# A hybrid decoder block on one core: five runs of small products a period, new engine orders, and three sums by ones as pairs of f32r products

## What is computed

```python
h = layer_norm(concat([meta, x]), ln_in_g, ln_in_b)
p = h @ w_in[l]
ya = rwkv7_branch(...)     # time mixer, 32 heads of 64
yb = pool_branch(...)      # causal pooling, windows 2, 4, 8, 16
merged = gate[:, :, 0] * (ya @ w_branch_a[l]) + gate[:, :, 1] * (yb @ w_branch_b[l])
h = layer_norm(DN_ALPHA * h + merged @ w_out[l], ln1_g[l], ln1_b[l])
h = layer_norm(DN_ALPHA * h + peer_ffn(h, ...), ln2_g[l], ln2_b[l])
```

```python
kk = kk / jnp.maximum(jnp.linalg.norm(kk, axis=-1, keepdims=True), 1e-12)
yv = jnp.mean(jnp.square(y - ym), axis=-1, keepdims=True)
bonus = jnp.sum(r_h * k_h * r_k, axis=-1, keepdims=True) * v_h
```

## Time and profile before

| | |
|---|---|
| median of 3 runs | 2405.33 us (2404.95 to 2405.37) |
| the profiled execution, its span | 2404.5 us |
| TensorE busy over the span | 2157.6 us (90%) |
| VectorE busy over the span | 1529.0 us (64%) |
| ScalarE busy over the span | 684.3 us (28%) |
| GpSimd busy over the span | 659.7 us (27%) |
| first and last transpose of V_st (`t`, once a pair) | 89.8 and 615.4 us |
| first product of the merge | 681.3 us |
| granted TensorE clock over the span | 0.992 of full |

### The profile page before, as it was taken

One profiled execution on the slowest core, in us unless ns is written; L12 is line 12 of the kernel. 1 busy time (PEld: TensorE's weight loads), 2 busy tenths in 40 slices (PEclk: granted clock), 3 DMA queues, 4 the chain that ended last, 5 costly groups with the idle time before them and its releaser, 6 DMA issues.

```text
span 2404.5 us, 37848 instructions
## 1 busy us (share of the span) xinstructions
PE 2157.6 (90%) x15331; PEld 1510.5 (63%) x15331; DVE 1529.0 (64%) x2605; ACT 684.3 (28%) x1366; POOL 659.7 (27%) x539
## 2 busy tenths in 40 slices
PE   9999999999999999998999889978877787777776
PEld 8999999999899999987554444433332233222222
DVE  7778888888765455548876567667446444444445
ACT  6555555455344444432121111111011000000000
POOL 1000000000000000004554555555455445444442
PEclk9999999999999999999999999999999999999999
DMA  6533333333367666679999999999999999999997
GB/s 213 141 95 98 102 88 101 103 88 98 106 184 194 185 187 187 190 270 342 417 427 424 425 423 426 427 427 426 427 427 428 426 427 427 427 427 427 427 427 289
DMA packets 348320, 708.19 MB, mean 295 GB/s; under 512 B 13834, under 2 KB 272482, under 8 KB 281826
## 3 DMA queue, kind: packets, MB, share of 16 engines
q0 software_dynamic: 74176, 537.01, 53.1%
q1 hardware_dynamic: 273732, 168.55, 24.1%
q10 hardware_dynamic: 240, 0.22, 0.0%
HBM read 703.63 MB, written 2.10 MB: 294 GB/s over the span
## 4 chain that ended last, share of the span: by engine, by line
DMA 36%; PE 17%; issue 2%; DVE 2%; POOL 1%; DVEq 0%; ACT 0%; POOLq 0%; ACTq 0%
DMA query_w<-in_v_table,experts 17%; DMA rows<-in_v_table,experts 13%; PE bank L1980 7%; PE project L1980 4%; DMA rows<-in_u_table,experts 3%; DMA up_rows<-in_u_table,experts 3%; PE bank L247 2%; DMA down_row_more<-in_v_table,experts 2%; PE bank L1896 2%; PE project L247 1%; PE bank L1938 0%; PE bank L1944 0%; PE bank L1612 0%; PE bank L1923 0%; POOL rows L1851 0%
## 5 line engine op out<-in xcount | busy, mean ns | idle before, releaser
L2102 DVE CUSTOM_DVE_ANT_0 rows<-rows,h 128x2048 f32<-128x2048 f32 x170 | 388.7, 2292 | 329.7 <-DMA rows<-in_u_table,experts 329.5
L1851 POOL DMA_INDIRECT rows<-in_u_table,experts x170 | 182.9, 1076 | 1097.7 <-DVE experts L1449 1040.0
L232 DVE TENSOR_TENSOR w_half_rest<-w_half,w_half_high 128x1024 fp32r<-128x1024 f32 x224 | 271.4, 1219 | 160.5 <-ACT w_half_high L211 160.3
L247 PE MATMUL project<-hT_high,w_half_high 128*128 128x272 f32 (+1 forms) x1152 | 351.1, 305 | 0.4 <-PEq L254 0.3
L1980 PE MATMUL bank<-query_w,merged_spare 128*128 128x512 f32 x608 | 283.6, 602 | 60.7 <-DMA query_w<-in_v_table,experts 47.3
L1980 PE MATMUL bank<-rows,merged_spare 128*128 128x512 f32 x612 | 286.4, 605 | 57.2 <-DMA rows<-in_v_table,experts 43.8
L247 PE MATMUL project<-hT,w_half_high 128*128 128x272 f32 (+1 forms) x1152 | 329.2, 286 | 0.0
L247 PE MATMUL project<-hT_high,w_half_rest 128*128 128x272 f32 (+1 forms) x1152 | 328.7, 285 | 0.0
L2102 DVE CUSTOM_DVE_ANT_0 up_rows<-up_rows,h 128x2048 f32<-128x2048 f32 x86 | 197.0, 2292 | 168.7 <-DMA up_rows<-in_u_table,experts 168.7
L211 ACT CAST w_half_high<-w_half 128x1024 fp32r<-128x1024 f32 x224 | 234.9, 1051 | 204.3 <-PE merge_ps L247 120.6
L1980 PEld LDWEIGHTS bank<-rows,merged_spare 128*128 128x128 f32 x612 | 114.0, 192 | 223.2 <-issue 127.3
(11 more groups left out here) (435 smaller groups left out, 3760.3 us busy)
## 6 DMA issues: line engine op xcount, KB each, us to landing
w_half<-in_w_in SPq DMA_DIRECT2D x176, 512.0 KB, 4.1
w_half<-in_w_branch_a SPq DMA_DIRECT2D x32, 512.0 KB, 3.9
out_w<-in_w_out SPq DMA_DIRECT2D x16, 1024.0 KB, 5.6
w_half<-in_w_branch_b SPq DMA_DIRECT2D x16, 512.0 KB, 3.9
query_w<-in_w_q_peer SPq DMA_DIRECT2D x8, 1024.0 KB, 16.2
out_w<-in_w_q_peer SPq DMA_DIRECT2D x6, 1024.0 KB, 19.1
lora_weights<-in_w_in SPq DMA_DIRECT2D x4, 896.0 KB, 14.1
rows<-in_u_table,experts POOLq DMA_INDIRECT x170, 21.1
```

Source lines behind the costliest of these rows:

```text
L232: return eng.tensor_tensor(low.bitcast(F32R), x, high, ALU.subtract)
L247: mm = nc.tensor.matmul(out, a.bitcast(F32R), b.bitcast(F32R), start=start and n == 0, stop=stop and n == 2)
L1851: pool.indirect_dma_start(ur[n % RU], None, w["u_table"][0], bass.IndirectOffsetOnAxis(ap=k.idx[:, t, h, j:j + 1], axis=0)).then_inc(s_u[n ...
L2102: v.tensor_tensor_reduce(ur[n % RU], ur[n % RU], k.h[:, n // (HEADS * TOPK), :], 1.0, 0.0, ALU.mult, ALU.add, dots(n, n + 1)).then_inc(s_d ...
```

## The change

Three things are done together.

1. *The three sums by ones.* `head_sums` makes each as two f32r products of a 128x128 matrix of ones, one with the rounded high part and one with the rest. ScalarE writes the high part (a second square in `sq` and `yc`, a copy in the new `bk`), VectorE the rest (`kq`, `br`, `gq`), and TensorE waits for the rest (`ksplit`, `rksplit`, `ysplit`).
2. *New orders for three engines.* TensorE has five runs of small products a period where it had seven. `u` of chunk c, `T` and `s` now stand in one run; before, `u` closed a run and `s` opened the next. `gv` goes from the end of stage 3 to the next period, between `Z` and `lw`. `gr` is cut in two with `s` 4, `T` 5 and `t` between them. On VectorE `go` moves from ahead of `s` 0 to behind `T` 1; `e` 2 moves ahead of `s` 0, `e` 0 ahead of `s` 2.
3. *Work moved between engines.* Two affine steps go from VectorE to ScalarE (the second line of `lw`, the new `lt`), and the per-pair copies of the parameter vectors (`cv`, and the first line of `ge`) are gone: operations read `k.vec` itself.

The diff, cut to its core (of the orders one line each):

```diff
 PE_ORDER = (
-    ("t", 1, 2), ("rb", 0, 2), ("u", 0, 3), ("lw", 0, 1), ("f", 10, 0), ("s", 0, 3), ("Z", 1, 2), ("r", 1, 3), ("la", 0, 1),
+    ("t", 1, 2), ("u", 0, 3), ("Z", 1, 2), ("gv", 0, 4), ("lw", 0, 1), ("f", 10, 0),
...
 DVE_ORDER = (
+    ("go", 0, 4), ("split", 3, 0), ("la", 0, 1), ("s", 1, 3), ("r", 2, 3), ("T", 2, 2), ("gy", 0, 4), ("lk", 0, 1), ("kq", 0, 1), ("split", 4, 0), ("e", 0, 0),
...
+            def head_sums(out, high, rest):
+
+                nc.tensor.matmul(out, ones_high[:].bitcast(F32R), high.bitcast(F32R), start=True, stop=False)
+                return nc.tensor.matmul(out, ones_high[:].bitcast(F32R), rest.bitcast(F32R), start=False, stop=True)
...
             def nm(_, p, par):
                 wait(pe, q["sig"], p * 3 + 3)
-                wait(pe, q["ksq"], p + 1)
-                nc.tensor.matmul(low[:, 0:T], ones, sq[:, real], start=True, stop=True).then_inc(q["norm"], 1)
+                wait(pe, q["ones"], 1)
+                wait(pe, q["ksplit"], p + 1)
+                head_sums(low[:, 0:T], sq_high[:], sq_rest[:, real]).then_inc(q["norm"], 1)
...
-            def gr(_, p, par):
+                wait(pe, q["rksplit"], p + 1)
+                head_sums(low[:, 0:SEQ], rk_high[:], rk_rest[:, CH:TP]).then_inc(q["bonus"], 1)
+
+            def gr(i, p, par):
 
                 wait(pe, q["st"], p + 1)
-                wait(pe, q["kst"], p + 1)
-                wait(pe, q["Zst"], p * 5)
-                wait(pe, q["off"], p)
-                for n, lhs in ((0, bst), (2, kst)):
-                    for c in range(NCH):
-                        mm = by_head(inv[n][:, c * CH:(c + 1) * CH], lhs[:, c, :], ast[par][:, c, :])
-                    mm.then_inc(q["gram"], 1)
+                if i:
+                    wait(pe, q["kst"], p + 1)
+                    wait(pe, q["Zst"], p * 5)
+                else:
+                    wait(pe, q["off"], p)
+                for c in range(NCH):
+                    mm = by_head(inv[2 * i][:, c * CH:(c + 1) * CH], (bst, kst)[i][:, c, :], ast[par][:, c, :])
+                mm.then_inc(q["gram"], 1)
...
+                if c == 1:
                     wait(pe, q["vsqrt"], p)
...
             def gv(_, p, par):
-                wait(pe, q["sqr"], p + 1)
-                nc.tensor.matmul(var_ps, ones, ysq[:], start=True, stop=True).then_inc(q["var"], 1)
+                wait(pe, q["ysplit"], p + 1)
+                if p + 1 < PAIRS:
+                    wait(pe, q["Uc"], p * 5 + 6)
+                head_sums(var_ps, ysq_high[:], ysq_rest[:]).then_inc(q["var"], 1)
...
             def sq_(_, p, par):
                 wait(act, q["shifted"], p * 3 + 3)
                 wait(act, q["norm"], p)
-                nc.scalar.activation(sq[:, real], kx[par][:, real], ACT.Square, scale=cur[par][:, V_KK:V_KK + 1]).then_inc(q["ksq"], 1)
+                nc.scalar.activation(sq[:, real], kx[par][:, real], ACT.Square, scale=k.vec[:, V_KK, p:p + 1])
+                nc.scalar.activation(sq_high[:].bitcast(F32R), kx[par][:, real], ACT.Square, scale=k.vec[:, V_KK, p:p + 1]).then_inc(q["ksq"], 1)
+
+            def bk(_, p, par):
+                wait(act, q["bonus"], p)
+                wait(act, q["rk"], p + 1)
+                nc.scalar.copy(rk_high[:].bitcast(F32R), rk[:, CH:TP]).then_inc(q["rkr"], 1)
 
             def lw(_, p, par):
                 wait(act, q["csum"], p)
                 wait(act, q["lora_mm"], p * 3 + 1)
-                nc.scalar.activation(sg[:, real], low[:, 0:T], ACT.Tanh, scale=0.5, bias=cur[par][:, V_W0H:V_W0H + 1]).then_inc(q["sig"], 1)
+                nc.scalar.activation(sg[:, real], low[:, 0:T], ACT.Tanh, scale=0.5, bias=k.vec[:, V_W0H, p:p + 1]).then_inc(q["sig"], 1)
+                wait(act, q["sig"], p * 3 + 1)
+                nc.scalar.activation(sg[:, real], sg[:, real], ACT.Copy, scale=0.5, bias=0.5).then_inc(q["sg"], 1)
...
+            def lt(_, p, par):
+                wait(act, q["rk"], p)
+                wait(act, q["sig"], p * 3 + 2)
+                nc.scalar.activation(t1[:, real], am[:, real], ACT.Identity, scale=k.vec[:, V_KAH, p:p + 1],
+                                     bias=k.vec[:, V_KAC, p:p + 1]).then_inc(q["rate"], 1)
...
             def y(_, p, par):
                 wait(act, q["done"], p)
                 wait(act, q["Yo"], p * 4 + 4)
-                nc.scalar.activation(ysq[:], y_ps, ACT.Square).then_inc(q["sqr"], 1)
+                nc.scalar.activation(ysq[:], y_ps, ACT.Square)
+                nc.scalar.activation(ysq_high[:].bitcast(F32R), y_ps, ACT.Square).then_inc(q["sqr"], 1)
                 nc.scalar.copy(yc[:], y_ps).then_inc(q["Yc"], 1)
...
+            nc.scalar.copy(ones_high[:].bitcast(F32R), ones).then_inc(q["ones"], 1)
...
-            def cv(_, p, par):
-                d()
-                n.tensor_copy(cur[par][:], k.vec[:, :, p]).then_inc(q["rm"], 1)
+            def kq(_, p, par):
+                wait(dve, q["ksq"], p + 1)
+                rest_bits(n, sq_rest[:, real], sq[:, real], sq_high[:]).then_inc(q["ksplit"], 1)
+
+            def br(_, p, par):
+                wait(dve, q["rkr"], p + 1)
+                rest_bits(n, rk_rest[:, CH:TP], rk[:, CH:TP], rk_high[:]).then_inc(q["rksplit"], 1)
+
+            def gq(_, p, par):
+                wait(dve, q["sqr"], p + 1)
+                rest_bits(n, ysq_rest[:], ysq[:], ysq_high[:]).then_inc(q["ysplit"], 1)
...
             def la(_, p, par):
-                wait(dve, q["sig"], p * 3 + 1)
-                n.tensor_scalar(sg[:, real], sg[:, real], 0.5, 0.5, ALU.mult, ALU.add)
-                d()
+                wait(dve, q["sg"], p + 1)
                 n.tensor_tensor_scan(cs[:, real], k.const[:, C_SCAN + PAD:C_SCAN + TP], sg[:, real], 0.0, ALU.mult, ALU.add)
-                wait(dve, q["sig"], p * 3 + 2)
-                n.tensor_scalar(t1[:, real], am[:, real], cur[par][:, V_KAH:V_KAH + 1], cur[par][:, V_KAC:V_KAC + 1], ALU.mult, ALU.add)
                 d()
                 n.tensor_tensor(csm[:, real], cs[:, real], sg[:, real], ALU.subtract).then_inc(q["csum"], 1)
 
             def lk(_, p, par):
-                d()
+                wait(dve, q["rate"], p + 1)
                 n.tensor_tensor(k2[:, real], kx[par][:, real], t1[:, real], ALU.mult)
                 d()
-                n.scalar_tensor_tensor(out=rk[:, CH:TP], in0=r[par][:, CH:TP], scalar=cur[par][:, V_RK:V_RK + 1], in1=k2[:, CH:TP],
+                n.scalar_tensor_tensor(out=rk[:, CH:TP], in0=r[par][:, CH:TP], scalar=k.vec[:, V_RK, p:p + 1], in1=k2[:, CH:TP],
                                        op0=ALU.mult, op1=ALU.mult).then_inc(q["rk"], 1)
...
             def ge(_, p, par):
-                n.tensor_copy(gcur[:], k.vec[:, V_GNG:V_GNB + 1, p])
                 if p == PAIRS - 1:
                     window(6)
...
             def go(_, p, par):
                 d()
-                n.scalar_tensor_tensor(out=yc[:], in0=yc[:], scalar=gcur[:, 0:1], in1=rstd[:], op0=ALU.mult, op1=ALU.mult)
+                n.scalar_tensor_tensor(out=yc[:], in0=yc[:], scalar=k.vec[:, V_GNG, p:p + 1], in1=rstd[:], op0=ALU.mult, op1=ALU.mult)
                 d()
-                n.scalar_tensor_tensor(out=yc[:], in0=yc[:], scalar=gcur[:, 1:2], in1=bon[p % 3][:], op0=ALU.add, op1=ALU.add)
+                n.scalar_tensor_tensor(out=yc[:], in0=yc[:], scalar=k.vec[:, V_GNB, p:p + 1], in1=bon[p % 3][:], op0=ALU.add, op1=ALU.add)
                 d()
```

More of the change, by code:

```diff
@@ L653, in rwkv_stage @@
         ww2, wa2, wg2 = sb("w_decay2", [DECAY_LORA, P]), sb("w_rate2", [ICL_LORA, P]), sb("w_gate2", [P, 2, P])
-        cur, gcur, eps = two("pair_vectors", [P, NVEC]), sb("pair_norm_vectors", [P, 2]), sb("group_norm_eps", [P, 1])
+        eps, ones_high = sb("group_norm_eps", [P, 1]), sb("ones_high", [P, P])
+        sq_high, rk_high, ysq_high = sb("k_square_high", [P, T]), sb("r_k_prod_high", [P, SEQ]), sb("y_square_high", [P, SEQ])
         r, kx, v = two("r", [P, TP]), two("k", [P, TP]), two("v", [P, TP])
@@ L659, in rwkv_stage @@
         pe_, pi, pm = sb("decay_prod", [P, TP]), sb("decay_prod_inv", [P, TP]), sb("decay_prod_prev", [P, TP])
-        kn, sq, rn = sb("k_for_norm", [P, TP]), sb("k_square", [P, TP]), sb("k_rnorm", [P, TP])
-        k2, t1, rk = sb("k_mixed", [P, TP]), sb("k_scale", [P, TP]), sb("r_k_prod", [P, TP])
+        kn, rn, sq_at = sb("k_for_norm", [P, TP]), sb("k_rnorm", [P, TP]), k.next_at()
+        sq, sq_rest = sb("k_square", [P, TP]), k.over("k_square_rest", [P, TP], sq_at)
+        k2, t1, rk_at = sb("k_mixed", [P, TP]), sb("k_scale", [P, TP]), k.next_at()
+        rk, rk_rest = sb("r_k_prod", [P, TP]), k.over("r_k_prod_rest", [P, TP], rk_at)
         gate, bon = three("gate", [P, SEQ]), three("bonus", [P, SEQ])
@@ L673, in rwkv_stage @@
         rhs, u, spc, s = sb("rhs", [P, CH]), sb("U", [P, CH]), sb("S_decayed", [P, CH]), two("S", [P, CH])
-        yc, ysq, rstd = sb("y", [P, SEQ]), sb("y_square", [P, SEQ]), sb("y_rstd", [P, SEQ])
```

(15 more changed lines are left out.)

6 lines of the change are left out of this document (2 added, 4 removed), and 29 rows, old and new, of tables (ACT_ORDER, DVE_ORDER, PE_ORDER).

## The result

The changed kernel takes 2479.5 us (median; 2472.9 to 2484.7) against 2405.4 before: a ratio of 1.0305, 95% interval 1.0281 to 1.0329. It is slower by 74 us where 5 were forecast, and far outside the range. The profiled execution is the slowest of the four: it took 2484.7 us, its span is 2482.9.

What follows compares the result with a forecast made beforehand. TensorE's queue was taken to set the mixer's pace. Full periods +2.7, ramp −3.3, last two periods −0.7, −0.4 and +1.0, last pair +5.5 sum to +4.8 us: 2410 us against the median 2405.33, range 2393 to 2417.

Steps and rivals of the forecast that it cites:

- S 3 to `Z` 5 and on to the next S 0: 0.4 and 0.9 idle: VectorE late in a mixer period: its work leaves 0.4 and 0.9 us idle in these two stretches.
- The forecast stall: TensorE's product with S of chunk 1 waits about 1.2 us for VectorE, in 13 periods; bounds 0 and 1.5.
- The gains on TensorE: Per mixer period: 0.42 us from the sums and 0.70 from five runs for seven, 1.12 us off TensorE.
- The step from the f32r variance back to `lw`: TensorE's return to fp32 on the same full array after `gv`: taken as 0.05 us, bounds nothing and 0.14.
- The three periods without `go`: The ramp: the first three periods keep the gain, 1.1 us faster each, 3.3 us in all.
- The end: Last two periods and last pair: 0.7 and 0.4 us saved, 1.0 and 5.5 us lost before the merge.
- The windows in `e` 2: Pooling windows ahead of S 0 near the stage's end: TensorE waits some 1.4 us, costing 1.0 more than before.
- my walk: Step-by-step sum behind the last pair's y, through window, reciprocal and split: merge at 683.2 instead of 681.28 us.
- C: Rival: a second stall, S 2 to S 3 or late U, 0.4 us a period, giving 2416 us; chance 0.15.
- A: Rival: VectorE's cover holds at the product with S of chunk 1, 2394 us (2388 without end cost); chance 0.20.
- D: Rival: the ramp gains nothing because the first pair's chain is longer, giving 2413 us; chance 0.08.
- B: Rival: effects cancel; chunk 1 stall about 0.8 us for 1.2 as VectorE's steps overlap more, 2405 us; chance 0.17.

Runs made afterwards that it cites:

- e1: The changed kernel with one number changed: `rs` waits for the outputs of the pair three back, not two back; 2419.7 us, ratio 1.0051.
- e2: The changed kernel, all waits kept, with five unread fp32 products on TensorE between `s` 4 and `T` 5; 2464.0 us, ratio 1.0238.
- e3: e1 with VectorE's `split 3` moved from between S 0 and S 1 to behind `T` 2; 2409.3 us, ratio 1.0010.
- e8: e6 with ScalarE's copy of U of chunk 1 moved ahead of `e` 0 and `ge`; 2401.4 us, ratio 0.9977.
- e7: e3 with all three sums by ones as single fp32 products again, without their high parts and rests; 2411.9 us, ratio 1.0022.
- e5: e3 with pooling window 6 moved, in the last pair, from ahead of VectorE's reciprocal to behind `gy`; 2408.5 us, ratio 1.0007.
- e6: e5 with the two length-4 windows moved from `e` 2 to `e` 1 of the period before; 2404.2 us, ratio 0.9990.

## Why the prediction was wrong, point by point

**The step that failed** is "S 3 to `Z` 5 and on to the next S 0: 0.4 and 0.9 idle". I added up VectorE's work between S 3 and `Z` 5 with `rs` at its duration and left out what `rs` waits for. The diff does not touch that line; the new order of TensorE moved the releaser (`s` 4) behind `Z` 5, whose result VectorE delivers after `rs`. With that wait removed (e1) the period is 35.6, for which I had 35.5. The wait cost 2.7 us a period of itself, some 40 of the 60 us between the changed kernel and e1.

**The second failure** is that I priced a wait at its own length. The forecast counted with the full clock throughout. With 2.5 us of idleness a period TensorE's clock dropped to its lower level with the wait or just behind it, in ten of 14 periods; e2, which leaves the wait and fills the time, is 15 us faster, some 20 without what its filling costs in two periods. That is the other part of the 60 us.

**The forecast stall was right**, nearly to the hundredth. In the kernel after, `s` 0 and the product with S of chunk 1 on TensorE, then S 0 and S 1 on VectorE:

```profile
405.99 0.33 PE L715 MATMUL invert<-BKV_by_token 64*64 64x64 f32 x4
...
412.92 0.33 PE L715 MATMUL chain<-S,A_st 64*64 64x64 f32 x4 [0.77 <-DVE S L1196]
```

```profile
204.78 0.28 DVE L1198 TENSOR_SCALAR S<-invert,chunk_decay 128x64 f32<-128x64 f32 x1 [1.21 <-PE invert L715]
...
210.88 0.28 DVE L1196 SCALAR_TENSOR_TENSOR S<-invert,chunk_decay,S_decayed 128x64 f32<-128x64 f32 x1
```

6.93 us from `s` 0 to the product, as summed; 6.10 us from S 0 to S 1, where the sum had 6.09. This was no luck: the steps between agree one by one (`split 3` starts 4.14 us behind `s` 0 for the summed 4.12, the scan 5.27 for 5.26). Only its price was too high: the product stands 0.77 us in its row and not 1.2, and 1.14 us of work taken out gave 0.82 (e3), because ScalarE's copy of U held `s` 1 back by 0.2 to 0.4 ahead of it. With that wait gone too (e8) the period is 1.1 below that of e1. The steps with their drains came out as in the earlier trace rows: 206.95 to 207.51 in the kernel after is 0.56 for a duration of 0.49. The sentence of the Trainium skill that the prediction set against this (VectorE: DVE Perf Modes, The DRAIN you can't avoid) speaks of semaphores between operations, which cost nothing extra; the rows have an explicit drain instruction, so they neither bear it out nor refute it, and no run here tests it.

**The gains on TensorE were right.** The sums give 0.22 for k (0.21 forecast) and 0.35 a period in all (0.42, e7 less e3). The step from the f32r variance back to `lw`, bounded by nothing and 0.14, costs nothing: in e1 the second product of the sum starts at 405.82 and `lw` at 405.94, the usual 0.12. This fits what the Trainium skill says (TensorEngine Tiling (Array Packing), Key Properties: a change of the tiling mode drains TensorE), since the mode does not change here. The three periods without `go` gained 2.8 us for the forecast 3.3: 0.8 from the first product of the projection to the first transpose of V_st (42.1 for 42.9), then 0.9 and 1.2 (e1: 29.6 for 30.5, 34.15 for 35.3). In the kernel after the third of them has the wait of `rs` already and takes 38.35.

**The end was right in kind and too small.** Forecast +5.4 (1.0 and 5.5, less 1.1 for fewer boundaries); measured 10.6 in the kernel after and 10.3 in e1. In order of time of the kernel after, TensorE and then VectorE:

```profile
719.58 0.33 PE L715 MATMUL chain<-S,A_st 64*64 64x64 f32 x4 [2.37 <-DVE S L1198]
...
741.88 0.28 PE L715 MATMUL chain<-RBKT_st,U 64*64 64x64 f32 x4
743.45 0.38 PE L775 MATMUL chain<-y_square_high,ones_high 128*128 128x256 f32 x1 [1.28 <-DVE y_square_rest L232]
...
749.19 0.55 PE L247 MATMUL project<-hT_high,w_half_high 128*128 128x256 f32 x1 [5.25 <-DVE w_half_rest L232]
...
758.15 0.35 PE L247 MATMUL merge_ps<-yaT_high,w_half_high 128*128 128x256 f32 x1 [0.32 <-PEq L649]
```

```profile
746.22 1.75 DVE L1207 RECIPROCAL y_rstd<-y_rstd 128x256 f32<-128x256 f32 x1
747.89 1.16 DVE L232 TENSOR_TENSOR w_half_rest<-w_half,w_half_high 128x1024 fp32r<-128x1024 f32 x1
```

Up to y 2.1 us are missing. The windows in `e` 2 were to make TensorE wait 1.4 us for S 0, 1.0 more than before; it waits 2.37, 2.1 more (0.27 before), and behind that wait the clock is low for 3.4 us.

Behind y, by my walk, the projection goes on 6.9 us later and the merge starts at 13.1; it is 7.2 and 16.2. The chain of VectorE is right; the last 16 units, for which the walk had 6.3 us to the merge, take 9.0, with the clock low behind the wait:

```profile
750.00:758.00 8.00, 7.83 (x46) 7.62 (x45) 3.28 (x5) 2.40 (x3) 0.00 (x0) 0.67 0.46 131
```

The same 16 units take 9.0, 8.7, 9.0, 8.3 and 7.7 us in the kernel after, e3, e5, e6 and e7, with 6.1, 5.2, 6.0, 4.8 and 3.7 us of it at half the clock. Less half of that time, all five are 5.9 to 6.1. So the excess here is the clock: the same failure as above, in a second place.

**The rivals.** The one that came true in kind is C, a second stall, with a chance of 0.15, but in another place and with 2.7 us a period for its 0.4. A (the cover holds) is refuted by the 6.10 us, and D (the ramp gains nothing) by the 2.8. B has about the stall that the row shows, 0.77, but not by its reason: VectorE's steps did not overlap more, TensorE came later. Two sums of the prediction are off by little: 13 periods of 0.23 are 3.0 and not 2.7, and rival A carries the end at 6.1 where the forecast's own terms make 5.4. The range came from the bounds of the costs that I knew of. Neither of its ends stood for a wait that I had not listed.

## What to carry to other kernels

When an order written by hand changes, list for each engine every wait of the code, not only of the units that moved, and find where its releaser stands now: the dangerous ones are those whose row shows a wait of a tenth or two before (here R_st, which waited 0.2 us a period for TensorE before the change), since they are just in time. A wait that asks for more than its buffers need is worth mending before any reordering. Price a repeated wait of TensorE like those here (2.0 to 2.5 us, once or twice a period) higher than its length, by what the clock then takes from the work behind it, and look at the granted clock of every variant.
